# A first norm in VectorE's own chain, and half-array products of two heads in alternation

## The chip, the cores and the metric

The kernel runs on 1 core of one Trainium2 chip. The metric is the device time of one execution in microseconds (us), lower is better. The times before are the median of 3 runs.

## What is computed

One sequence of 256 tokens with 1024 features goes through two transformer blocks in float32. The parts that matter here:

```
x1 = x + 0.5 * g0 * swiglu(modulate(x, norm_w[0], shift, scale), w13, w2)   # first norm, first FFN
...
o = causal_mla_attention(...)      # first attention: 8 heads, value width 64, 256 tokens
...
y_a = mixer_a(qa, ka, va, ...)     # second attention: 8 heads of width 128
y_b = mixer_b(qb, kb, vb, bias)    # last attention: 4 heads x 3 dilations, width 64, with a bias table
x = x + (gate_a * y_a @ w_out_a + gate_b * y_b @ w_out_b) @ w_out
...                                # an MLP, a gated embedding, a last norm
```

modulate is `rmsnorm(x) * w * (1 + scale) + shift`, where scale and shift are products of silu(c) with the matrix w_ada. All weights, some 210 MB, are read once from HBM.

## The kernel before

A class `Plan` writes one list of steps by hand for the whole program; each engine then walks this list and issues those steps that are its own. An engine works its instructions strictly in that order and waits on semaphores. So the order of the plan is the order of each engine.

Weights come in units of 1 MB (128 x 2048 floats) into 4 slots `sb_raw`. A unit of kind "w" is split: ScalarE writes the rounded high part to `sb_ring` (step `hi`, two halves), VectorE the remainder (step `lo`), and a slot is loaded again as soon as its `lo` is done. TensorE multiplies each 128 x 128 tile in three passes (high x high, high x low, low x high). A unit of kind "ada" holds two blocks of columns of w_ada; VectorE multiplies it by `sb_csil` (silu of c) and sums into `sb_mod` (step `ada`, twice a unit, 128x1024 each, into `sb_junk`).

**The start** (`first_ffn`). ScalarE squares the 8 tiles of x (`square_0`), VectorE adds them (`sb_acc`), and between two of the squares, at the places in `SILU_AT`, ScalarE computes `silu_c` of each half of c. Then come unit 0 (ada), the norm of x (`x_norm`: TensorE sums over features; VectorE makes mean + eps in `sb_nst`; three Newton steps of 1/sqrt; two diagonal matrices in `sb_tq`), units 1 (w) and 2 (ada), and `norm_rows` (TensorE spreads the factors, ScalarE copies them to `sb_rbc`). With the argument `on_pool` true, the Newton steps and the diagonals are GpSimd's (POOL), else VectorE's. For each k of 8 follow `acol` (1 + scale times the norm's weight), `xr` = x times rbc (VectorE), `h_hi` (ScalarE, two instructions: scale and shift, then the rounded copy), `h_lo` (VectorE), and 16 tiles (48 matmuls 128x256) of TensorE. From k = 1 on each k also takes one w unit and one ada unit.

**The attentions** run in steps between tiles of other products: a step comes every `STEP_1` = 7 tiles (21 matmuls) in the first attention and every `STEP_B` = 12 tiles (36 matmuls) in the last. `in_steps` has 8 heads in four stages, and step n holds, in this order, the division of head n-1 (`normal`), scores of head n, the transposes of head n-2 (`turn_1`, `turn_pB`), and the product with values of head n-3 (`pv_1`, `pv_B`). Between these stages VectorE adds mask or bias (`masked_1`, `biased_B`), ScalarE takes the exponential and copies the transposes out of PSUM (`turned_1`, `turned_pB`). All transposes of one attention use one PSUM bank. These products are in full float32: one instruction in the code is two passes on the array. The values' products write 64 of 128 partitions (weights of 64 columns), the upper half for odd heads; scores of the last attention contract over 64 rows, again the upper half for odd heads. `load_bias(1)` brings the bias tables of heads 4 to 7 of the last attention (R<-scratch, two DMAs of 768 KB) into the place of the first ones and therefore waits for `biased_B` of head 3.

Of the kernel before, what the change touches and what calls it, by code (L numbers as in the profile page):

```python
# [20 lines left out]
LATE = 2  # L21
SILU_AT = (4, 7)
Z_SCALE = -8192.0
# [412 lines left out]
class Plan:  # L436
# [205 lines left out]
    def first_ffn(self):  # L642
# [22 lines left out]
        self.flush()  # L665
        norm = self.x_norm("f1", True)
        for _ in range(2):
            self.take_unit()
            self.flush()
        self.norm_rows(norm)  # L670
        bk = [b.take() for b in B]
        for k in range(8):
            if k > 1:
                self.take_unit()
                self.flush()
            if k:
# [36 lines left out]
    def mixer_1(self):  # L713
# [158 lines left out]
        def attention():  # L872
            for src in range(2):
                for hp in range(4):
# [4 lines left out]
                    done(b, ("turned", src, hp))  # L879
            p_b, pt_b, o_bank = {}, {}, [None]  # L880

# [17 lines left out]
            def pv(h):  # L899
                if h % 2 == 0:  # L900
                    o_bank[0] = B[7].take()
                pt = pt_b.pop(h)
                self.add("pv_1", h, o_bank[0], pt)
                done(pt, ("pv_1", h))
                if h % 2:
                    self.add("o_hi_1", h // 2, o_bank[0])
                    self.fill()
                    self.add("o_lo_1", h // 2, o_bank[0])
                    done(o_bank[0], ("o_1", h // 2))

# [60 lines left out]
    def mixer_2(self):  # L971
# [111 lines left out]
        def attention_b():  # L1083
            def scores(n):
                b, s, p = B[4 + n % 2].take(), tmp.take(), tmp.take()
                self.add("scores_B", n, b)
                self.add("biased_B", n, b, s)
                done(b, ("biased_B", n))
                self.add("exp_B", n, s, p)
                done(s, ("exp_B", n))  # L1090
                p_b[n] = p
                if n == 3:
                    self.add("load_bias", 1)

            o_bank = [None]

            def pv(n):
                t, s = divmod(n, 4)
                if s == 0:
                    o_bank[0] = B[7].take()  # L1100
                pt = pt_b.pop(n)
                self.add("pv_B", n, o_bank[0], pt)
                done(pt, ("pv_B", n))
# [261 lines left out]
class Tensor(Program):  # L1365
# [202 lines left out]

    def pv_1(self, h, o_bank, pt):
        m, e = self.m, self.e  # L1570
        if h % 2 == 0:
            self.turn(o_bank)
            e.wait_ge(*self.at("v_out", 1))
        e.wait_ge(*self.at("turned_1", h))
        o = o_bank.ap[64 * (h % 2):64 * (h % 2) + 64, :]
        e.matmul(o[:, 0:256], m.v1(0)[:, 64 * h:64 * h + 64], pt.ap[:, 0:256], True, False)
        e.matmul(o[:, 128:256], m.v1(1)[:, 64 * h:64 * h + 64], pt.ap[:, 256:384], False, True).then_inc(
            *self.up("pv1_ready", ("pv_1", h)))

# [72 lines left out]

    def scores_b(self, n, b):
        m, e = self.m, self.e
        t, s = divmod(n, 4)
        self.turn(b)
# [3 lines left out]
        rows = slice(64 * (s % 2), 64 * (s % 2) + 64)  # L1660
        for g in range(3):
            a = 2 * g + s // 2
            k = m.KB()[rows, a, :] if g == 0 else m.KB()[rows, a, 128 * t:128 * t + 128]
            o = b.ap[:, 0:256] if g == 0 else b.ap[:, 128 + 128 * g:256 + 128 * g]
            ins = e.matmul(o, m.QB()[rows, a, 128 * t:128 * t + 128], k, g == 0, True)
        ins.then_inc(*self.up("scoresB_ready", ("scores_B", n)))
# [8 lines left out]

    def pv_b(self, n, o_bank, pt):
        m, e = self.m, self.e
        t, s = divmod(n, 4)
        if s == 0:
# [3 lines left out]
        e.wait_ge(*self.at("turned_pB", n))  # L1683
        c = 256 * (s // 2) + 128 * t
        o = o_bank.ap[64 * (s % 2):64 * (s % 2) + 64, c:c + 128]
        vs = [m.vB(0)[:, 64 * s:64 * s + 64], m.vB(1)[:, 64 * s:64 * s + 64],
              m.vB(t)[:, 64 * (4 + s):64 * (4 + s) + 64], m.vB(t)[:, 64 * (8 + s):64 * (8 + s) + 64]]
        for i in range(4):
            ins = e.matmul(o, vs[i], pt.ap[:, 128 * i:128 * i + 128], i == 0, i == 3)
        ins.then_inc(*self.up("pvB_ready", ("pv_B", n)))  # L1690
# [76 lines left out]
class Scalar(Program):  # L1767
# [61 lines left out]
    def h_hi(self, k):  # L1829
        m, e = self.m, self.e  # L1830
        xr = m.reg(44 + k, 256)
        e.wait_ge(*self.at("xr", k))
        e.wait_ge(*self.at("acol", 0, k))
        e.wait_ge(*self.at("ada", k))
        e.activation(xr, xr, FN.Identity, scale=m.acol[:, k:k + 1], bias=m.mod[:, k:k + 1]).then_inc(
            *self.up("scalar_own"))
        e.wait_ge(*self.last())
        e.activation(m.hk(k)[0], xr).then_inc(*self.up("h_hi", ("h_hi", k)))

# [161 lines left out]
    def o_hi_1(self, hp, bank):  # L2001
        e = self.e
        e.wait_ge(*self.at("pv_1", 2 * hp + 1))
        e.activation(self.m.pair(28 + 2 * hp)[0], bank.ap[:, 0:T]).then_inc(*self.up("o_hi", ("o_hi_1", hp)))
# [103 lines left out]
    def o_hi_b(self, t, o):  # L2108
        m, e = self.m, self.e
        c = slice(128 * t, 128 * t + 128)  # L2110
        e.wait_ge(*self.at("pv_B", 4 * t + 3))
        e.activation(m.OB(0)[:, :, c], o.ap.rearrange("p (a n) -> p a n", a=2)[:, :, c]).then_inc(
# [103 lines left out]
class Vector(Elementwise):  # L2216
# [117 lines left out]

# [423 lines left out]
    def biased_b(self, n, b, s):  # L2758
# [4 lines left out]
        e.wait_ge(*self.at("bias", t, 1))  # L2763
        e.wait_ge(*self.at("scores_B", n))
        for g in range(3):
# [329 lines left out]
```

## Time and profile before

| | before |
|---|---|
| median of 3 runs | 1047.17 us (1046.88 to 1048.25) |
| the profiled execution | 1046.66 us, of which 1044.5 us are its span |
| PE (TensorE) busy | 1004.4 us, 96% |
| DVE (VectorE) busy | 758.7 us, 73% |
| ACT (ScalarE) busy | 533.8 us, 51% |
| POOL (GpSimd) busy | 17.5 us |
| DMA | 215.09 MB |

The span runs from the first to the last instruction of the profiled execution. Times in the rows below are us from the span's start; PEld is TensorE's loading of weights.

### The profile page before, as it was taken

How to read it: one execution, taken by the hardware profiler on the slowest of the kernel's cores; microseconds unless marked ns; L12 is line 12 of the kernel's file. 1: busy time of each engine (PE TensorE's matmuls, PEld its weight loads, DVE VectorE, ACT ScalarE, POOL GpSimd, SP SyncE). 2: the span in 40 equal slices, each digit the busy share in tenths (PEclk: the TensorE clock that was granted, in tenths of full speed). 3: DMA queues.
4: the chain of work that ended last, by engine and by line, in shares of the span. 5: the costliest groups of instructions: out<-in, count | busy, mean ns of one | idle time of the engine just before them, and what ended most of it. 6: DMA issues, size and time to landing. Idle time of an engine off the chain costs nothing.

```text
span 1044.5 us, 18951 instructions
## 1 busy us (share of the span) xinstructions
PE 1004.4 (96%) x7848; PEld 969.2 (93%) x7848; DVE 758.7 (73%) x1387; ACT 533.8 (51%) x920; POOL 17.5 (2%) x47
## 2 busy tenths in 40 slices
PE   2999999998889999999999999999999999999996
PEld 1999999997887999999999988799899999999996
DVE  4978998878976787685775598547568855565675
ACT  4544654436376555354564445655345654355443
POOL 2000000003000000000000000000000000000000
PEclk9999999999999999999999999999999999999998
DMA  8878899764573554678765436356554554556411
GB/s 332 321 288 304 310 353 353 291 200 163 177 267 121 201 200 165 240 230 214 249 225 193 163 121 220 140 156 172 140 181 161 178 196 166 198 181 208 152 68 41
DMA packets 34532, 215.09 MB, mean 206 GB/s; under 512 B 3725, under 2 KB 7693, under 8 KB 9614
## 3 DMA queue, kind: packets, MB, share of 16 engines
q1 hardware_dynamic: 34446, 213.88, 59.3%
q8 instruction: 62, 1.02, 0.4%
q14 instruction: 24, 0.20, 0.1%
HBM read 211.25 MB, written 2.62 MB: 205 GB/s over the span
## 4 chain that ended last, share of the span: by engine, by line
PE 85%; DVE 6%; ACT 4%; DMA 2%; issue 2%; POOL 2%; SPq 0%; DVEq 0%; ACTq 0%; POOLq 0%
PE bank L210 83%; PE bank L213 1%; DVE sb_ring L189 1%; ACT sb_ring L186 1%; ACT sb_tmp L186 1%; DMA R<-scratch 1%; ACT R L186 1%; DVE sb_tq L189 1%; DVE sb_tmp L189 1%; DVE sb_junk L198 1%; DVE sb_tmp L195 0%; POOL sb_nst L189 0%; DMA sb_x<-xt 0%; DMA sb_raw<-wts 0%; DVE sb_tmp L198 0%
## 5 line engine op out<-in xcount | busy, mean ns | idle before, releaser
L210 PE MATMUL bank<-sb_h,sb_ring 128*128 128x256 f32 (+2 forms) x4224 | 521.4, 284 | 8.1 <-DVE sb_ring L189 4.1
L210 PEld LDWEIGHTS bank<-sb_h,sb_ring 128*128 128x128 f32 (+1 forms) x4224 | 511.2, 189 | 12.1 <-issue 5.3
L189 DVE TENSOR_TENSOR sb_ring<-sb_raw,sb_ring 128x1024 fp32r<-128x1024 f32 x322 | 385.0, 1211 | 3.9 <-ACT sb_ring L186 3.8
L186 ACT ACTIVATE sb_ring<-sb_raw 128x1024 fp32r<-128x1024 f32 x322 | 319.8, 1042 | 108.6 <-PE bank L210 60.5
L210 PE MATMUL bank<-R_512r,sb_ring 128*128 128x256 f32 x1920 | 234.6, 283 | 0.0
L210 PEld LDWEIGHTS bank<-R_512r,sb_ring 128*128 128x128 f32 x1920 | 231.0, 189 | 0.8 <-issue 0.7
L189 DVE TENSOR_TENSOR sb_tq<-bank,sb_rbc 128x256 f32<-128x256 f32 x107 | 43.0, 421 | 95.0 <-PE bank L210 52.3
L198 DVE CUSTOM_DVE_ANT_0 sb_junk<-sb_raw,sb_csil,sb_cols 128x1024 bf16<-128x1024 f32 x72 | 92.3, 1281 | 1.8
L210 PE MATMUL bank<-R_1024r,sb_ring 128*128 128x256 f32 x768 | 91.5, 281 | 0.0
L210 PEld LDWEIGHTS bank<-R_1024r,sb_ring 128*128 128x128 f32 x768 | 91.3, 188 | 0.0
L210 PE MATMUL bank<-sb_ring,sb_h 128*128 128x512 f32 (+1 forms) x384 | 89.8, 387 | 0.0
L210 PEld LDWEIGHTS bank<-sb_ring,sb_h 128*128 128x128 f32 x384 | 68.1, 188 | 13.5
L186 ACT ACTIVATE R_512r<-sb_tq 128x256 fp32r<-128x256 f32 x60 | 25.1, 418 | 77.4 <-DVE sb_tq L189 50.3
L186 ACT ACTIVATE sb_tmp<-bank 128x512 f32<-128x512 f32 (+2 forms) x46 | 25.6, 561 | 41.2 <-PE bank L210 38.1
L186 ACT ACTIVATE sb_tmp<-sb_tmp,sb_smx 128x256 f32<-128x256 f32 (+2 forms) x40 | 20.9, 524 | 44.3 <-DVE sb_smx L198 33.9
L189 DVE TENSOR_TENSOR sb_tmp<-sb_tmp 128x512 f32<-128x512 f32 (+2 forms) x24 | 15.3, 638 | 31.4 <-ACT sb_tmp L186 31.2
L186 ACT ACTIVATE sb_h<-sb_x,sb_cols 128x256 fp32r<-128x256 f32 x24 | 14.2, 592 | 43.6 <-DVE sb_x L195 21.9
L195 DVE SCALAR_TENSOR_TENSOR sb_x<-bank,sb_gcol,sb_x 128x256 f32<-128x256 f32 x24 | 11.6, 482 | 34.2 <-PE bank L210 34.1
L186 ACT ACTIVATE sb_tq<-sb_tq,sb_zb 128x256 f32<-128x256 f32 x26 | 13.3, 510 | 32.3 <-DVE sb_tq L189 32.3
L189 DVE TENSOR_TENSOR R_512r<-sb_tq,R_512r 128x256 fp32r<-128x256 f32 x60 | 25.2, 420 | 3.9 <-ACT R_512r L186 3.9
L213 PE MATMUL bank<-sb_con,sb_tmp 128*128 128x128 f32 (+1 forms) x134 | 21.3, 277 | 5.2 <-ACT sb_tmp L186 3.0
L210 PE MATMUL bank<-R,R 128*128 128x256 f32 (+5 forms) x114 | 24.9, 344 | 0.0
(152 smaller groups left out, 546.8 us busy)
## 6 DMA issues: line engine op xcount, KB each, us to landing
sb_raw<-wts SPq DMA_DIRECT2D x194, 1024.0 KB, 5.1
R<-scratch SPq DMA_DIRECT2D x4, 768.0 KB, 7.8
scratch<-R SPq DMA_DIRECT2D x1, 1536.0 KB
sb_x<-xt SPq DMA_DIRECT2D x2, 512.0 KB, 5.3
out<-R SPq DMA_DIRECT2D x2, 512.0 KB, 2.9
sb_raw<-wts SPq DMA_DIRECT2D x1, 768.0 KB, 4.3
sb_raw<-wts SPq DMA_DIRECT2D x1, 640.0 KB, 4.2
sb_raw<-wts SPq DMA_DIRECT2D x1, 512.0 KB, 3.6
```

Source lines behind the costliest of these rows:

```text
L186: return Issued(self.e and self.e.activation(o, i, func, **kw))
L189: return Issued(self.e and self.e.tensor_tensor(*a))
L195: return Issued(self.e and self.e.scalar_tensor_tensor(*a))
L198: return Issued(self.e and self.e.tensor_tensor_reduce(*a))
L210: return Issued(self.e and self.e.matmul(o, w, m, start=start, stop=stop, skip_group_check=True))
L213: return Issued(self.e and self.e.transpose(o, i, ident))
```

## The change

Three things change, and the program computes the same.

First, the start. `x_norm("f1")` is called without `on_pool`, so the Newton steps and diagonals of the first norm are VectorE's; unit 2 (ada) is taken after k = 0 and no longer before `norm_rows`; `silu_c` comes ahead of square 0 and square 3; `xr` multiplies by `acol` too, `h_hi` is one instruction that only adds the shift, and `h_lo` adds the shift again before it subtracts.

```diff
-SILU_AT = (4, 7)
+SILU_AT = (0, 3)
...
-        norm = self.x_norm("f1", True)
-        for _ in range(2):
-            self.take_unit()
-            self.flush()
+        norm = self.x_norm("f1")
+        self.take_unit()
+        self.flush()
         self.norm_rows(norm)
...
-            if k > 1:
+            if k:
                 self.take_unit()
                 self.flush()
-            if k:
                 self.take_unit()
...
     def h_hi(self, k):
-        e.activation(xr, xr, FN.Identity, scale=m.acol[:, k:k + 1], bias=m.mod[:, k:k + 1]).then_inc(
-            *self.up("scalar_own"))
-        e.wait_ge(*self.last())
-        e.activation(m.hk(k)[0], xr).then_inc(*self.up("h_hi", ("h_hi", k)))
+        e.activation(m.hk(k)[0], m.reg(44 + k, 256), FN.Identity, bias=m.mod[:, k:k + 1]).then_inc(
+            *self.up("h_hi", ("h_hi", k)))
...
     def xr(self, k):
-        e.tensor_tensor(m.reg(44 + k, 256), m.x[:, k, :], m.rbc, ALU.mult).then_inc(*self.up("xr", ("xr", k)))
+        e.scalar_tensor_tensor(m.reg(44 + k, 256), m.x[:, k, :], m.acol[:, k:k + 1], m.rbc, ALU.mult,
+                               ALU.mult).then_inc(*self.up("xr", ("xr", k)))
...
     def h_lo(self, k):
-        e.tensor_tensor(lo, m.reg(44 + k, 256), hi.bitcast(F32), ALU.subtract).then_inc(
-            *self.up("h_lo", ("h", "f1", k)))
+        e.scalar_tensor_tensor(lo, m.reg(44 + k, 256), m.mod[:, k:k + 1], hi.bitcast(F32), ALU.add,
+                               ALU.subtract).then_inc(*self.up("h_lo", ("h", "f1", k)))
```

Second, `pv_1` and `pv_B` are issued for two heads at once, in the odd head's place (steps 4, 6, 8 and 10), and alternate between the two halves of columns.

```diff
             def pv(h):
-                if h % 2 == 0:
-                    o_bank[0] = B[7].take()
-                pt = pt_b.pop(h)
-                self.add("pv_1", h, o_bank[0], pt)
-                done(pt, ("pv_1", h))
                 if h % 2:
+                    o = B[7].take()
+                    pts = [pt_b.pop(h - 1), pt_b.pop(h)]
+                    self.add("pv_1", h // 2, o, pts)
...
-        for i in range(4):
-            ins = e.matmul(o, vs[i], pt.ap[:, 128 * i:128 * i + 128], i == 0, i == 3)
+        for i in range(4):
+            v = m.vB(i if i < 2 else t)
+            for side, pt in enumerate(pts):
+                s = 2 * a + side + (0 if i < 2 else 4 * (i - 1))
+                ins = e.matmul(o_bank.ap[64 * side:64 * side + 64, c:c + 128], v[:, 64 * s:64 * s + 64],
+                               pt.ap[:, 128 * i:128 * i + 128], i == 0, i == 3)
```

Third, `scores_B` is issued for two heads at once, in the even head's place (steps 0, 2, 4 and 6), into two banks, and alternates between the halves of rows.

```diff
             def scores(n):
-                b, s, p = B[4 + n % 2].take(), tmp.take(), tmp.take()
-                self.add("scores_B", n, b)
+                if n % 2 == 0:
+                    s_b.update({n: B[4].take(), n + 1: B[5].take()})
+                    self.add("scores_B", n // 2, s_b[n], s_b[n + 1])
+                b, s, p = s_b.pop(n), tmp.take(), tmp.take()
...
         for g in range(3):
+            i = 2 * g + a
+            for side, b in enumerate(banks):
+                rows = slice(64 * side, 64 * side + 64)
...
+                ins = e.matmul(o, m.QB()[rows, i, 128 * t:128 * t + 128], k, g == 0, True)
```

VectorE's instructions at the start, before, from the last row of unit 0's `ada` (`ISA sb_mod`) to the low part of h for k = 0:

```order
L198 ISA sb_mod 128x1
L192 TENSOR_SCALAR sb_nst<-bank 128x2
L189 TENSOR_TENSOR sb_ring<-sb_raw,sb_ring 128x1024 x2
L198 ISA sb_junk,sb_mod<-sb_raw,sb_csil,sb_cols 128x1024
L198 ISA sb_mod 128x1
L198 ISA sb_junk,sb_mod<-sb_raw,sb_csil,sb_cols 128x1024
L198 ISA sb_mod 128x1
L195 SCALAR_TENSOR_TENSOR sb_acol<-sb_mod,sb_cols 128x1
L189 TENSOR_TENSOR R_256_53<-sb_x,sb_rbc 128x256
L189 TENSOR_TENSOR sb_h<-R_256_53,sb_h 128x256
```

And VectorE in the same place with the change (R_256_53 is the product of `xr` for k = 0):

```order
L192 TENSOR_SCALAR sb_nst<-bank 128x2
L192 TENSOR_SCALAR sb_nst<-sb_nst 128x2
L189 TENSOR_TENSOR sb_nst<-sb_nst 128x2 x2
L195 SCALAR_TENSOR_TENSOR sb_nst<-sb_nst 128x2
L189 TENSOR_TENSOR sb_nst<-sb_nst 128x2 x2
L195 SCALAR_TENSOR_TENSOR sb_nst<-sb_nst 128x2
L189 TENSOR_TENSOR sb_nst<-sb_nst 128x2 x2
L195 SCALAR_TENSOR_TENSOR sb_nst<-sb_nst 128x2
L192 TENSOR_SCALAR sb_tq<-sb_con,sb_nst 128x128 x2
L189 TENSOR_TENSOR sb_ring<-sb_raw,sb_ring 128x1024 x2
L195 SCALAR_TENSOR_TENSOR sb_acol<-sb_mod,sb_cols 128x1
L195 SCALAR_TENSOR_TENSOR R_256_53<-sb_x,sb_acol,sb_rbc 128x256
```

The ten small instructions of 1/sqrt and the two diagonals came in ahead of unit 1's `lo`, and the two `ada` of unit 2 went out of this place (to behind k = 0).

TensorE's instructions in steps 3 and 4 of the last attention, before (R_1536_101 and R_1536_102 are the keys and queries of `scores_B`, `L213` the transposes of `turn_pB`, R_768_103 and R_768_104 the values of `pv_B`, the others the tiles between the steps):

```order
L210 MATMUL bank<-R_1536_101,R_1536_102 128x256
L210 MATMUL bank<-R_1536_101,R_1536_102 128x128 x2
L213 MATMUL bank<-sb_con,sb_tmp 128x128 x4
L210 MATMUL bank<-sb_tmp,R_768_103 64x128
L210 MATMUL bank<-sb_tmp,R_768_104 64x128
L210 MATMUL bank<-sb_tmp,R_768_103 64x128 x2
L210 MATMUL bank<-R_512r,sb_ring 128x256 x12
L210 MATMUL bank<-sb_h,sb_ring 128x256 x24
L210 MATMUL bank<-R_1536_101,R_1536_102 128x256
L210 MATMUL bank<-R_1536_101,R_1536_102 128x128 x2
L213 MATMUL bank<-sb_con,sb_tmp 128x128 x4
```

TensorE in steps 3 and 4 with the change:

```order
L213 MATMUL bank<-sb_con,sb_tmp 128x128 x4
L210 MATMUL bank<-R_512r,sb_ring 128x256 x12
L210 MATMUL bank<-sb_h,sb_ring 128x256 x24
L210 MATMUL bank<-R_1536_101,R_1536_102 128x256 x2
L210 MATMUL bank<-R_1536_101,R_1536_102 128x128 x4
L213 MATMUL bank<-sb_con,sb_tmp 128x128 x4
L210 MATMUL bank<-sb_tmp,R_768_103 64x128 x2
L210 MATMUL bank<-sb_tmp,R_768_104 64x128 x2
L210 MATMUL bank<-sb_tmp,R_768_103 64x128 x4
```

Step 3 keeps its transposes alone; step 4 has the scores of heads 4 and 5 and the values' products of heads 0 and 1. Head 3's scores moved from step 3 to step 2.

## Rows read from the trace of the kernel before

**Rows 1.** Page, part 1: busy time, share and instructions of each engine.

```profile
PE 1004.4 (96%) x7848; PEld 969.2 (93%) x7848; DVE 758.7 (73%) x1387; ACT 533.8 (51%) x920; POOL 17.5 (2%) x47
```

**Rows 2.** Timeline of the start, all engines: start, duration, engine, what.

```profile
11.00 1.28 DVE L198 CUSTOM_DVE_ANT_0 sb_junk<-sb_raw,sb_csil,sb_cols 128x1024 bf16<-128x1024 f32 x1
...
13.39 2.00 ACT L186 ACTIVATE sb_ring<-sb_raw 128x1024 fp32r<-128x1024 f32 x2 [2.43 <-DMA sb_raw<-wts]
...
13.53 0.15 DVE L192 TENSOR_SCALAR sb_nst<-bank 128x2 f32<-128x2 f32 x1
...
14.48 2.36 DVE L189 TENSOR_TENSOR sb_ring<-sb_raw,sb_ring 128x1024 fp32r<-128x1024 f32 x2 [0.80 <-ACT sb_ring L186]
...
21.26 0.73 POOL L192 TENSOR_SCALAR sb_tq<-sb_con,sb_nst 128x128 f32<-128x128 f32 x2 [0.18 <-POOL sb_nst L189]
...
21.68 1.22 PE L210 MATMUL bank<-sb_tq,sb_con 128*128 128x128 f32 x4 [8.68 <-POOL sb_tq L192]
22.94 0.38 ACT L186 ACTIVATE sb_rbc<-bank 128x256 f32<-128x256 f32 x1 [7.55 <-PE bank L210]
...
24.52 0.42 ACT L186 ACTIVATE sb_h<-R 128x256 fp32r<-128x256 f32 x1
...
24.97 0.43 DVE L189 TENSOR_TENSOR sb_h<-R,sb_h 128x256 fp32r<-128x256 f32 x1 [1.11 <-ACT sb_h L186]
...
25.50 36.67 PE L210 MATMUL bank<-sb_h,sb_ring 128*128 128x256 f32 x289 [2.59 <-issue]
```

**Rows 3.** Windows: busy us (instructions) of PE, PEld, DVE, ACT, POOL; PEclk; DMA; GB/s.

```profile
25.50:29.86 4.36, 4.36 (x20) 4.36 (x21) 4.21 (x7) 4.14 (x6) 0.00 (x0) 1.00 0.11 26
...
33.50:45.00 11.50, 11.50 (x98) 11.50 (x98) 11.36 (x19) 5.92 (x9) 0.00 (x0) 1.00 0.99 371
```

**Rows 4.** Timeline of VectorE in the next norm: first and last of its chain.

```profile
402.70 0.16 DVE L192 TENSOR_SCALAR sb_nst<-bank 128x2 f32<-128x2 f32 x1 [0.55 <-PE bank L210]
...
404.86 0.48 DVE L192 TENSOR_SCALAR sb_tq<-sb_con,sb_nst 128x128 f32<-128x128 f32 x2
```

**Rows 5.** Groups by shape, VectorE: count, busy us, mean ns.

```profile
L195 DVE SCALAR_TENSOR_TENSOR sb_h<-sb_x,sb_acol,sb_h 128x256 fp32r<-128x256 f32 x16 | 7.7, 483 | 7.4 <-ACT sb_h L186 7.3
```

**Rows 6.** Timeline of TensorE, last attention: scores, step 5's transposes, last product.

```profile
707.16 1.14 PE L210 MATMUL bank<-R,R 64*128 64x256 f32 x6
...
712.69 1.14 PE L210 MATMUL bank<-R,R 64*128 64x256 f32 x6
...
718.24 1.14 PE L210 MATMUL bank<-R,R 64*128 64x256 f32 x6
...
724.15 1.14 PE L210 MATMUL bank<-R,R 64*128 64x256 f32 x6
...
731.30 1.14 PE L210 MATMUL bank<-R,R 64*128 64x256 f32 x6
...
740.30 0.66 PE L213 MATMUL bank<-sb_con,sb_tmp 128*128 128x128 f32 x4 [0.72 <-ACT sb_tmp L186]
...
766.85 1.09 PE L210 MATMUL bank<-sb_tmp,R 128*64 128x128 f32 x8 [0.16 <-ACT sb_tmp L186]
```

**Rows 7.** Timeline of TensorE in the first attention, steps 4 and 6.

```profile
321.20 0.55 PE L213 MATMUL bank<-sb_con,sb_tmp 128*128 128x128 f32 x3 [0.80 <-ACT sb_tmp L186]
321.68 0.86 PE L210 MATMUL bank<-sb_tmp,R 128*64 128x256 f32 x4
322.47 2.78 PE L210 MATMUL bank<-sb_h,sb_ring 128*128 128x258 f32 x21
...
330.68 0.55 PE L213 MATMUL bank<-sb_con,sb_tmp 128*128 128x128 f32 x3 [0.28 <-ACT sb_tmp L186]
```

**Rows 8.** Timeline of ScalarE ahead of step 5 of the first attention.

```profile
324.99 0.17 ACT L186 ACTIVATE sb_zb<-bank 128x1 f32<-128x1 f32 x1 [1.15 <-PE bank L210]
```

**Rows 9.** Timeline of the DMA queue (SPq): the second load of bias.

```profile
727.07 1.28 SPq L216 DMA_DIRECT2D R<-scratch  x2
```

**Rows 10.** Timeline of VectorE: the first use of that bias.

```profile
737.28 0.61 DVE L198 CUSTOM_DVE_ANT_1 sb_tmp<-bank,R 128x256 f32<-128x256 f32 x1 [5.04 <-DMA R<-scratch]
```

More of the change, by code:

```diff
@@ L879, in attention @@
                     done(b, ("turned", src, hp))
-            p_b, pt_b, o_bank = {}, {}, [None]
+            p_b, pt_b = {}, {}
             def scores(h):
@@ L899, in pv @@
             def pv(h):
-                if h % 2 == 0:
-                    o_bank[0] = B[7].take()
-                pt = pt_b.pop(h)
-                self.add("pv_1", h, o_bank[0], pt)
-                done(pt, ("pv_1", h))
-                if h % 2:
-                    self.add("o_hi_1", h // 2, o_bank[0])
+                if h % 2:
+                    o = B[7].take()
+                    pts = [pt_b.pop(h - 1), pt_b.pop(h)]
+                    self.add("pv_1", h // 2, o, pts)
+                    for pt in pts:
+                        done(pt, ("pv_1", h // 2))
+                    self.add("o_hi_1", h // 2, o)
                     self.fill()
-                    self.add("o_lo_1", h // 2, o_bank[0])
-                    done(o_bank[0], ("o_1", h // 2))
+                    self.add("o_lo_1", h // 2, o)
+                    done(o, ("o_1", h // 2))
             yield from in_steps(scores, lambda h: self.add("normal_1", h, p_b[h]), turn, pv)
@@ L1093, in scores @@
                     self.add("load_bias", 1)
-            o_bank = [None]
+            o_bank, s_b = [None], {}
             def pv(n):
@@ L1100, in pv @@
                     o_bank[0] = B[7].take()
-                pt = pt_b.pop(n)
-                self.add("pv_B", n, o_bank[0], pt)
-                done(pt, ("pv_B", n))
+                if s % 2:
+                    pts = [pt_b.pop(n - 1), pt_b.pop(n)]
+                    self.add("pv_B", n // 2, o_bank[0], pts)
+                    for pt in pts:
+                        done(pt, ("pv_B", n // 2))
                 if s == 3:
@@ L1567, in turn_1, with pv_1 @@
         e.transpose(b.ap[:, 256:384], p.ap[:, 128:256], m.ident).then_inc(*self.up("p1_turned", ("turn_1", h)))
-    def pv_1(self, h, o_bank, pt):
+    def pv_1(self, hp, o, pts):
         m, e = self.m, self.e
[L1571 to L1578, printed above, removed]
+        self.turn(o)
+        e.wait_ge(*self.at("v_out", 1))
+        e.wait_ge(*self.at("turned_1", 2 * hp + 1))
+        for part in range(2):
+            for i, pt in enumerate(pts):
+                h, a = 2 * hp + i, o.ap[64 * i:64 * i + 64, :]
+                if part == 0:
+                    e.matmul(a[:, 0:256], m.v1(0)[:, 64 * h:64 * h + 64], pt.ap[:, 0:256], True, False)
+                else:
+                    ins = e.matmul(a[:, 128:256], m.v1(1)[:, 64 * h:64 * h + 64], pt.ap[:, 256:384], False, True)
+        ins.then_inc(*self.up("pv1_ready", ("pv_1", hp)))
     def branch(self, f, k, bank):
@@ L1651, in pv_a, with scores_b @@
             *self.up("pvA_ready", ("pv_A", h)))
-    def scores_b(self, n, b):
+    def scores_b(self, n, *banks):
         m, e = self.m, self.e
-        t, s = divmod(n, 4)
-        self.turn(b)
+        t, a = divmod(n, 2)
+        self.turn(*banks)
         for what in ("kB0", "kqB", "qB0"):
@@ L1659, in scores_b @@
             e.wait_ge(*self.at("turned_2", (what, 1)))
-        rows = slice(64 * (s % 2), 64 * (s % 2) + 64)
         for g in range(3):
[L1662 to L1665, printed above, removed]
+            i = 2 * g + a
+            for side, b in enumerate(banks):
+                rows = slice(64 * side, 64 * side + 64)
+                k = m.KB()[rows, i, :] if g == 0 else m.KB()[rows, i, 128 * t:128 * t + 128]
+                o = b.ap[:, 0:256] if g == 0 else b.ap[:, 128 + 128 * g:256 + 128 * g]
+                ins = e.matmul(o, m.QB()[rows, i, 128 * t:128 * t + 128], k, g == 0, True)
         ins.then_inc(*self.up("scoresB_ready", ("scores_B", n)))
@@ L1674, in turn_pb, with pv_b @@
         ins.then_inc(*self.up("pB_turned", ("turn_pB", n)))
-    def pv_b(self, n, o_bank, pt):
+    def pv_b(self, n, o_bank, pts):
         m, e = self.m, self.e
-        t, s = divmod(n, 4)
-        if s == 0:
+        t, a = divmod(n, 2)
+        if a == 0:
             self.turn(o_bank)
@@ L1682, in pv_b @@
             e.wait_ge(*self.at("vB_out", "v1", 1))
[L1683 to L1687, printed above, removed]
-        for i in range(4):
-            ins = e.matmul(o, vs[i], pt.ap[:, 128 * i:128 * i + 128], i == 0, i == 3)
+        e.wait_ge(*self.at("turned_pB", 2 * n + 1))
+        c = 256 * a + 128 * t
+        for i in range(4):
+            v = m.vB(i if i < 2 else t)
[3 more added lines that the diff above has]
+                               pt.ap[:, 128 * i:128 * i + 128], i == 0, i == 3)
         ins.then_inc(*self.up("pvB_ready", ("pv_B", n)))
@@ L2002, in o_hi_1 @@
         e = self.e
-        e.wait_ge(*self.at("pv_1", 2 * hp + 1))
+        e.wait_ge(*self.at("pv_1", hp))
         e.activation(self.m.pair(28 + 2 * hp)[0], bank.ap[:, 0:T]).then_inc(*self.up("o_hi", ("o_hi_1", hp)))
@@ L2110, in o_hi_b @@
         c = slice(128 * t, 128 * t + 128)
-        e.wait_ge(*self.at("pv_B", 4 * t + 3))
+        e.wait_ge(*self.at("pv_B", 2 * t + 1))
         e.activation(m.OB(0)[:, :, c], o.ap.rearrange("p (a n) -> p a n", a=2)[:, :, c]).then_inc(
@@ L2325, in xr @@
         e.wait_ge(*self.at("rbc", "f1"))
-        e.tensor_tensor(m.reg(44 + k, 256), m.x[:, k, :], m.rbc, ALU.mult).then_inc(*self.up("xr", ("xr", k)))
+        e.wait_ge(*self.at("acol", 0, k))
+        e.scalar_tensor_tensor(m.reg(44 + k, 256), m.x[:, k, :], m.acol[:, k:k + 1], m.rbc, ALU.mult,
+                               ALU.mult).then_inc(*self.up("xr", ("xr", k)))
     def h_lo(self, k):
@@ L2763, in biased_b @@
         e.wait_ge(*self.at("bias", t, 1))
-        e.wait_ge(*self.at("scores_B", n))
+        e.wait_ge(*self.at("scores_B", n // 2))
         for g in range(3):
```

2 lines of the change are left out of this document (removed).

## The prediction

> **What bounds the kernel now.** I read the page first, then a table of windows, then the timeline at the three changed places. TensorE is busy for 1004.4 of 1044.5 us [rows 1], so the end moves by what TensorE's stream gains or loses, and by nothing else. Some 40 us are idle for TensorE, and the largest single stretch is the start: its main products begin at 25.50 [rows 2] and from then on run without a gap through the first FFN. That start is the one place where another engine's chain counts in full. In the attentions the question is of two sorts: how long TensorE's own half-array blocks take, and whether it then stands before a result that is not there yet.
>
> **The start, before.** The chain is to be seen in [rows 2]. VectorE is through with unit 0's two ada and makes the variance at 13.53. GpSimd then takes until 21.26 to come to the diagonals. TensorE's spread at 21.68 had waited for them, ScalarE copies rbc at 22.94, and xr, two instructions of h_hi (the last at 24.52) and h_lo (24.97 to 25.40) follow. Meanwhile unit 1's lo (14.48) was long done.
>
> **The start, after.** What comes first stays where it is. Putting silu ahead lets the squares end earlier, but unit 1 lands only at 13.39 (ScalarE had waited 2.43 for it), units land one behind another, and at 371 GB/s [rows 3] a unit of 1.05 MB takes 2.8 us; so unit 0 lands at 10.6 or a little later, and its first ada can't start much ahead of the 11.00 of before. The variance stays at 13.5. I give silu's move 0, with at most 0.4 to gain.
> - VectorE's chain: in the next norm it is 2.16 us from the variance to the first diagonal (402.70 to 404.86), and 0.48 for both [rows 4]. So the first diagonal is at 15.7 and VectorE is free at 16.2.
> - Unit 1's lo: ScalarE has finished hi at 15.4, so lo runs from 16.1 for 2.36, to 18.5. The spread and rbc take from 21.68 to 23.32 before [rows 2], 1.64 us; after, they end at 17.4, beside lo. So lo is the longer of the two branches.
> - acol 0.1, xr as a three-operand instruction 0.48 [rows 5], h_hi 0.42 to 0.6, h_lo 0.48, and some 0.15 us of handing over: 1.65 us. TensorE begins at 20.15, against 25.50. This term is -5.35 us.
> - Does TensorE then keep going? Its first 20 matmuls took 4.36 us, 0.218 each, and later ones 98 in 11.50, 0.117 [rows 3], or, over the whole row of 289 in 36.67 us [rows 2] less these, 0.120; I take 0.119 for each. The granted clock reads 1.00 in both rows, so the row doesn't name the cause; the first pitch fits the lower of the two levels, 1.2 GHz, since TensorE had done nothing for 2.59 us before it. I expect this slow beginning again, unchanged, since it stands idle for some 3 us again. The 48 matmuls of k = 0 then end at 20.15 + 4.4 + 28 x 0.119 = 27.9. VectorE until then: ada twice 2.65, acol 0.1, xr 0.45, lo 2.3, h_lo 0.45, about 5.85 with what overlaps taken off, from 20.05 to 25.9. There are 2 us of slack at k = 1, where before unit 2 had been taken in advance. VectorE runs gapless there already (11.36 of 11.50 us) at TensorE's pace. Two three-operand instructions cost 0.06 us each more for every k, 0.12 x 7 = 0.8 us, less than the 2 us. DMA has its units issued in the same relation to their use as in the later k. So nothing is given back; if the slack failed, up to 2 us would be.
>
> **The half-array blocks.** In the last attention the distances in [rows 6] give each block's net cost. Scores and 36 matmuls: 712.69 - 707.16 = 5.53; 36 x 0.119 is 4.28, so scores of one head cost 1.25. With transposes 724.15 - 718.24 = 5.91, so these cost 0.38 to 0.44. With the values' product 731.30 - 724.15 = 7.15, so it costs 1.24. The product is 8 passes in 1.09 us, the last one's latency of some 0.3 included, so a pass of 128 columns takes 0.11 and one of 256 some 0.215. Pure passes are thus 0.88 of 1.24 and 0.87 of 1.25: about 0.37 us of each visit is spent on going from the whole array to half of it and back. In the first attention a product takes 0.79 from start to start (321.68 to 322.47 in [rows 7]), and 0.95 with what it costs on both sides.
>
> Two heads in one visit save 0.37 each time, a sure thing: 12 visits fewer, 4.4 us of TensorE time. The unknown is whether passes of different halves run at the same time. No row shows two halves back to back. Bounds: none, then a pair's passes take 1.74 (scores), 1.76 (values, last) or 1.30 (values, first); or full, with each head's second pass beside the other's first: 9 slots of 0.11 = 1.0 for 16 passes, 0.75 for the first attention; for scores I take 1.2, since a matrix of 128 columns must be loaded for each pass at the pitch of 0.117 that PEld shows [rows 3]. I take full, since the two heads' passes share no operand and write other partitions or another bank.
>
> The Trainium skill ("TensorEngine Tiling (Array Packing)", Key Properties) says that changing the tiling mode drains the engine and changing the tile alone doesn't, and that tiles can load and multiply in parallel; this agrees with the 0.37 us of a visit. But "TensorE: Matmul & The Clock Gate" (Part 3, The mechanism) says that a weight load overlaps with matmuls in flight only when the row group differs. Column halves share their rows, so by this rule alone only the scores would gain, and the sum would be 1041.0 instead of 1036.9.
>
> **What of this reaches the end.** First attention. Step 3 loses its product (-0.95), but at step 4 the transposes already wait 0.80 for ScalarE [rows 7], whose work up to there was released before step 3's product; so this goes into a wait of 1.75. Step 5 loses one, and step 6 waits already (0.28), behind ScalarE work that begins at 324.99, before step 5 [rows 8]; lost too. Steps 7 and 9 show no such wait, and their 1.9 us are gained, but for some 0.3 at step 9's transposes. The four pairs cost 0.37 + 0.75 = 1.1 against 0.95, +0.1 each. Sum: -1.2 us (+0.6 without overlap, when each pair costs 0.65 more than one product).
>
> Last attention. A pair of scores costs 0.4 + 1.2 = 1.6, a pair of products 0.35 + 1.0 = 1.35. From 707.16: step 1 at 713.05, step 2 at 717.35, step 3 at 723.7, step 4 at 728.45, step 5 at 736.1. But the second bias load stands there: issued at 727.07 [rows 9], used at 737.28, VectorE having waited 5.04 for it [rows 10], and ScalarE frees the transposes' bank only behind exp of that head, so TensorE's transposes of step 5 already wait 0.72, until 740.30. That load goes out after head 3's bias, which VectorE can add 0.9 us earlier (its scores are there), and takes its 10.2 us in any case. So the transposes come at 739.35: TensorE now waits 3.2 us, and of all that was won up to there only 0.95 reaches the end. From there: step 6 at 744.2, step 7 at 751.9, step 8 at 756.6, step 9 at 761.3. The last product needs ScalarE's copy of step 9's transposes, and waits for it before too (0.16 at 766.85 [rows 6]); transposes, copy and handing over come to some 1.8 us, so it starts at 763.1 and ends at 764.1, against 766.85 + 1.02 = 767.9. Sum: -3.75 us. Without overlap the same steps give 767.9, that is 0.
>
> **Sum.** -5.35 - 1.2 - 3.75 = -10.3 us against the profiled 1046.66, or 1036.4. The median of the runs is 0.5 above the profiled time: 1036.9.
>
> **The rivals.**
> - No overlap of halves at all: -5.35 + 0.6 + 0 = -4.75, 1042.4. For it: every pass in the rows keeps to 0.11, however small its half. Against it: nothing in the rows forces two halves into one queue. 0.18.
> - Row halves overlap and column halves don't, because the load of one head's 64 columns waits until the other head's pass is through: -5.35 + 0.6 - 1.4 (the bias load is met at the same 739.35, three pairs of products cost 0.8 more each) = -6.1, 1041.0. For it: products go through all 128 rows for both heads. Against it: 64-column loads are as hidden in the rows as others. 0.12. It is what the Trainium skill's rule in "TensorE: Matmul & The Clock Gate" (Part 3, The mechanism) would give.
> - The start gives most back: TensorE reaches k = 1 before VectorE does, or its slow beginning lasts longer because it has less work ahead. It costs 2 to 5 of the 5.35 us; with overlap 1040. For it: VectorE is busy 11.36 of 11.50 us. Against: the 2 us of slack. 0.08.
> - TensorE is slow again after the 3.2 us wait at step 5, as it is after its wait at 25.50: another 20 matmuls at 0.218, +2.0, 1038.9; inside the likeliest case's range.
> - Slower than before: going from half to half costs as much as going from whole to half, some 0.1 to 0.2 us. The pairs have 4 x (3 + 7 + 5) = 60 such changes. The -4.75 us of the case without overlap are used up at 0.08 us for each change; at 0.2 it is +7.3, 1054.4. Against it stands that a load of 64 columns for the next pass is already hidden within a visit. 0.04.
>
> **How the numbers follow.** The likeliest case, full overlap, has a chance of 0.58 and a range of its own of 1034.5 to 1039.5 (start 1.5 either way, the waits 1 either way, the slow stretch +2). The range reaches on to the cases without overlap, to 1042.7; above lie the slower case and a part of the third. Faster by over 0.2% (2.1 us, about what a measurement here can tell from nothing): 0.94. Within 0.2%: 0.02. Slower: 0.04.
>
> **What would show it.** In the profile of the changed kernel: no GpSimd row before 25 us; the variance at 13.5 and the first diagonal 2.2 us later; the first 128x256 matmul at 20 to 20.5, and none waiting for sb_ring or sb_h up to 60. A pair of values' products (16 passes) that starts and ends within 1.3 us, not 2.0; a pair of scores (12 passes) within 1.5, not 1.95. Steps 4 and 6 of the first attention with waits of 1.7 and 1.2 us for ScalarE, and step 5 of the last with 3 us behind R<-scratch. It is wrong if the pairs take the sum of their passes, if the first matmul comes after 21, or if TensorE starves at k = 1.

## The result, and the profile after

Before: 1047.03 us (median of 4 runs, 1046.35 to 1048.25). After: 1037.66 us (median of 4 runs, 1036.80 to 1038.82). The ratio is 0.9913, with a 95% interval of 0.9901 to 0.9924: 9.4 us faster. The profiled execution took 1037.56 us, with a span of 1035.8. The forecast was 1036.9. The single steps are off by more than the sum, as the rows show.

The page's line of busy times, which answers to [rows 1]:

```profile
span 1035.8 us, 18934 instructions
PE 993.6 (96%) x7848; PEld 962.9 (93%) x7848; DVE 761.8 (74%) x1399; ACT 528.8 (51%) x911; POOL 10.5 (1%) x32
```

TensorE issues as many matmuls as before and is busy 10.8 us less. The start, on the timeline of all engines, which answers to [rows 2] (start, duration, engine, line, operation; in brackets the idle time before it and what ended it):

```profile
10.69 1.28 DVE L198 CUSTOM_DVE_ANT_0 sb_junk<-sb_raw,sb_csil,sb_cols 128x1024 bf16<-128x1024 f32 x1 [0.36 <-DMA sb_raw<-wts]
...
13.23 0.15 DVE L192 TENSOR_SCALAR sb_nst<-bank 128x2 f32<-128x2 f32 x1
...
15.46 0.48 DVE L192 TENSOR_SCALAR sb_tq<-sb_con,sb_nst 128x128 f32<-128x128 f32 x2
...
15.86 2.35 DVE L189 TENSOR_TENSOR sb_ring<-sb_raw,sb_ring 128x1024 fp32r<-128x1024 f32 x2
17.06 0.38 ACT L186 ACTIVATE sb_rbc<-bank 128x256 f32<-128x256 f32 x1 [1.93 <-PE bank L210]
...
18.95 0.51 ACT L186 ACTIVATE sb_h<-R,sb_mod 128x256 fp32r<-128x256 f32 x1 [1.51 <-DVE R L195]
...
19.49 0.49 DVE L195 SCALAR_TENSOR_TENSOR sb_h<-R,sb_mod,sb_h 128x256 fp32r<-128x256 f32 x1 [0.58 <-ACT sb_h L186]
...
20.08 1.19 PE L210 MATMUL bank<-sb_h,sb_ring 128*128 128x256 f32 x4 [3.06 <-DVE sb_h L195]
```

GpSimd is gone from the stretch, 2.23 us lie between the variance and the first diagonal, unit 1's lo outlasts rbc, and the first main product is at 20.08, 5.42 us earlier. From xr to the first main product it is 1.65 us (18.43 to 20.08), and was 2.07 (23.43 to 25.50): of the 5.42 us, 0.42 come from the fewer instructions for h, and 5.00 from the chain ahead of xr. From the first main product to 233 us TensorE's record has no distance between two starts above 0.6 us: k = 1 doesn't starve it.

TensorE's timeline of the first attention (step 4 and step 6), answering to [rows 7], and of the last one, answering to [rows 6]:

```profile
315.68 0.55 PE L213 MATMUL bank<-sb_con,sb_tmp 128*128 128x128 f32 x3 [1.77 <-ACT sb_tmp L186]
316.16 0.87 PE L210 MATMUL bank<-sb_tmp,R 128*64 128x256 f32 x8
316.96 2.78 PE L210 MATMUL bank<-sb_h,sb_ring 128*128 128x258 f32 x21
...
325.16 0.55 PE L213 MATMUL bank<-sb_con,sb_tmp 128*128 128x128 f32 x3 [1.27 <-ACT sb_tmp L186]
...
700.53 1.15 PE L210 MATMUL bank<-R,R 64*128 64x256 f32 x12
...
722.65 1.09 PE L210 MATMUL bank<-sb_tmp,R 128*64 128x128 f32 x16
723.67 3.11 PE L210 MATMUL bank<-R_512r,sb_ring 128*128 128x256 f32 x24
726.62 1.58 PE L210 MATMUL bank<-sb_h,sb_ring 128*128 128x256 f32 x12
732.93 1.11 PE L213 MATMUL bank<-sb_con,sb_tmp 128*128 128x128 f32 x4 [4.73 <-ACT sb_tmp L186]
...
740.21 1.15 PE L210 MATMUL bank<-R,R 64*128 64x256 f32 x12
...
758.29 1.09 PE L210 MATMUL bank<-sb_tmp,R 128*64 128x128 f32 x16 [1.17 <-ACT sb_tmp L186]
759.31 3.11 PE L210 MATMUL bank<-sb_h,sb_ring 128*128 128x256 f32 x24
```

A pair now takes what one head took: 16 passes in 1.09 us where 8 took 1.09 [rows 6], 12 in 1.15, 8 in 0.87. But at step 5 TensorE stands idle for 4.73 us. VectorE's timeline shows the bias load behind it, and the table of windows what TensorE does ahead of it and afterwards, with the start's first matmuls in the first row (length; busy time and instructions of PE, PEld, DVE, ACT, POOL; granted clock; DMA share; GB/s):

```profile
729.84 0.60 DVE L198 CUSTOM_DVE_ANT_1 sb_tmp<-bank,R 128x256 f32<-128x256 f32 x1 [7.21 <-DMA R<-scratch]
```

```profile
20.08:24.60 4.52, 4.52 (x21) 4.52 (x22) 4.41 (x8) 1.78 (x3) 0.00 (x0) 1.00 0.80 274
...
726.00:728.10 2.10, 2.10 (x19) 2.00 (x17) 0.00 (x0) 0.00 (x0) 0.00 (x0) 1.00 1.22 230
731.54:738.37 6.83, 5.44 (x26) 5.44 (x27) 5.37 (x14) 4.89 (x9) 0.00 (x0) 0.50 0.34 114
732.90:737.50 4.60, 4.57 (x22) 4.57 (x23) 3.55 (x10) 2.77 (x4) 0.00 (x0) 0.50 0.32 91
732.93:740.21 7.28, 7.28 (x41) 7.15 (x41) 4.20 (x12) 3.53 (x6) 0.00 (x0) 0.63 0.41 146
```

Ahead of the wait at step 5 19 matmuls are under way in 2.10 us, at a granted clock of 1.00; behind it 22 take 4.57 at 0.50, which is 1.2 of 2.4 GHz. The clock fell at 731.54, while TensorE stood idle, and was back at 1.00 at 738.37. From the transposes to the next scores it takes 7.28 us. The 1.00 of the first row is no measurement: the trace's own records of the clock begin only at 24.98 us (before: 29.79), where the half pace of the start ends, and the table reads a stretch without a record as 1.00.

Where the 8.7 us of span come from, as shifts of TensorE's milestones: first main product -5.42; first attention's scores at 297.36 against 302.62; the attention itself 43.18 us against 45.01 (-1.83); 0.46 lost between the attentions; the last attention 58.78 against 60.71 (-1.93). The rest are hundredths on the way. The 0.46 come from a gap near 476 us in which TensorE starts nothing for 0.86 us; the profile names no releaser for it. The profiled executions of three kernels below have it too (0.7 to 0.9) and those of the kernel before and of six others don't, with and without the change; its cause stays open.

### The profile page after: what moved, and what is told of

It is laid out like the page before. It is cut to its first block, busy times and chain, and to the rows that moved or that the text cites. A ratio compares the mean times of both kernels' runs of the same rounds, so it can differ in the third digit from the quotient of the medians.

```text
span 1035.8 us, 18934 instructions
## 1 busy us (share of the span) xinstructions
PE 993.6 (96%) x7848; PEld 962.9 (93%) x7848; DVE 761.8 (74%) x1399; ACT 528.8 (51%) x911; POOL 10.5 (1%) x32
## 4 chain that ended last, share of the span: by engine, by line
PE 82%; DVE 8%; ACT 4%; DMA 3%; issue 2%; POOL 1%; SPq 0%; DVEq 0%; ACTq 0%; POOLq 0%
PE bank L210 81%; DVE sb_ring L189 2%; DMA R<-scratch 2%; PE bank L213 1%; ACT sb_ring L186 1%; DMA sb_raw<-wts 1%; ACT sb_tmp L186 1%; DVE sb_tmp L198 1%; DVE sb_tq L189 1%; ACT R L186 1%; DVE sb_tmp L189 1%; DVE sb_junk L198 1%; DVE sb_tmp L192 0%; DVE sb_tmp L195 0%; POOL sb_st_a L189 0%
## 5 line engine op out<-in xcount | busy, mean ns | idle before, releaser
L210 PEld LDWEIGHTS bank<-sb_ring,sb_h 128*128 128x128 f32 x384 | 68.1, 188 | 13.5
L213 PE MATMUL bank<-sb_con,sb_tmp 128*128 128x128 f32 (+1 forms) x134 | 21.7, 281 | 11.1 <-ACT sb_tmp L186 8.9
L213 PEld LDWEIGHTS bank<-sb_con,sb_tmp 128*128 128x128 f32 (+1 forms) x134 | 15.9, 143 | 15.9 <-ACT sb_tmp L186 9.6
```

The costliest lines, as they stand in the source:

```text
L210: return Issued(self.e and self.e.matmul(o, w, m, start=start, stop=stop, skip_group_check=True))
L213: return Issued(self.e and self.e.transpose(o, i, ident))
```

## Experiments

All are compared with the kernel before on the same chip.

**The start alone.** The kernel before with the whole first change: the norm in VectorE's chain, unit 2's ada later, silu ahead, fewer instructions for h. A cut of it:

```diff
-        norm = self.x_norm("f1", True)
-        for _ in range(2):
-            self.take_unit()
-            self.flush()
+        norm = self.x_norm("f1")
+        self.take_unit()
+        self.flush()
...
```

> The kernel before with the change at the start alone. Theory: the gain at the start is worth its full 5.4 us at the end, since TensorE has no gap behind it through the first FFN: first 128x256 matmul at 20.1 and 1041.6 us (ratio 0.9948). Rival: a part is given back later, where TensorE meets the same waits earlier (transfers keep their time): 1042.5 to 1044, with the loss seen at the start of the first or the last attention.

1040.86 us, ratio 0.9942 (0.9927 to 0.9957): 5.7 us faster, and 5.2 in span. First main product at 20.48, last attention 5.28 us earlier than before. Little is given back: the last attention takes 61.00 us instead of 60.71, with a wait of 1.00 instead of 0.72 at step 5.

**The pairs alone.** The changed kernel with the start's edits undone (the whole first change the other way round).

> The changed kernel with the start as it was before. Theory: the parts add, so this one has 1.8 us from the first attention and 1.9 from the last, and 0.4 to 1.3 that the 1.2 us of shift between them showed: 1043.3 to 1043.7 us (ratio 0.9967). First matmul back at 25.5, the wait for the second bias load at step 5 of the last attention still 4.5 to 5 us, and a slow stretch of TensorE behind it. Rival: part of what looked like the pairs' gain is the earlier start's, because transfers and other engines are then ahead: 1045 or more.

1043.56 us, ratio 0.9968 (0.9955 to 0.9981): 3.0 us faster. The first attention takes 43.47 us, the last 57.55; the wait at step 5 is 4.47, and from the transposes behind it to the next scores it takes 6.31. The first matmul, expected back at 25.5, comes at 26.41: in this execution VectorE's first ada already starts at 11.82 instead of 11.00, so the shift is there ahead of everything that the edit reaches, and no run names its cause. The two gains, 5.7 and 3.0, add to 8.7 of the 9.4, within what the intervals leave open.

**Two ada ahead of the norm's rows.**

```diff
         norm = self.x_norm("f1")
-        self.take_unit()
-        self.flush()
+        for _ in range(2):
+            self.take_unit()
+            self.flush()
         self.norm_rows(norm)
...
```

> The changed kernel, but with unit 2's ada taken on VectorE ahead of the first norm's rows, as before the change. Theory (with the norm in VectorE's own queue, whatever stands ahead of it there counts in full): two ada of 1.3 us each push the first 128x256 matmul from 20.08 to 22.7, and the time to 1040.3 us. Rival (unit 1's lo by VectorE, 15.86 to 18.2, is the longer branch anyway, and TensorE meets VectorE again at k = 1, where the ada taken early are missing): first matmul later, but less than 1 us lost at the end, 1038.5.

VectorE's and TensorE's rows on the timeline:

```profile
18.22 1.28 DVE L198 CUSTOM_DVE_ANT_0 sb_junk<-sb_raw,sb_csil,sb_cols 128x1024 bf16<-128x1024 f32 x1
...
22.71 2.69 PE L210 MATMUL bank<-sb_h,sb_ring 128*128 128x256 f32 x11 [5.59 <-DVE sb_h L195]
```

The first product comes 2.63 us later, as the theory said, and at 233 to 236 us and at the first attention's scores (299.65 against 297.36) TensorE is still 2.3 us behind the changed kernel. The time is 1039.22 (ratio 0.9923, 0.9906 to 0.9939), between the two forecasts and, beside 0.9913, not clearly apart from the changed kernel; this execution lacks the gap near 476 us that the changed kernel's has, and that hides 0.8 of the 2.3. The trace decides for the theory, the time of the runs alone would not.

**Silu at its old place.** One line, `SILU_AT = (4, 7)`.

> The changed kernel with silu at its old place behind the squares. Theory: the first ada starts at 11.0 instead of 10.7, and the first matmul at 20.4 instead of 20.08; +0.3 us. Rival (unit 0's landing sets the first ada, silu is early enough in both): the first matmul at 20.1.

The first ada starts at 10.87, the first product at 20.25, in one execution that took 1036.11. Kernels with silu ahead and the same start have it at 19.86 to 20.48. The 0.17 us to the changed kernel are within that scatter, so no effect can be told: 0 in the forecast fits.

**The pairs not alternated.** Same visits, the second head's matmuls behind all of the first's (shown for the last attention's products; scores and the first attention's products alike):

```diff
         for i in range(4):
-            v = m.vB(i if i < 2 else t)
-            for side, pt in enumerate(pts):
+        for side, pt in enumerate(pts):
+            for i in range(4):
+                v = m.vB(i if i < 2 else t)
...
```

> The changed kernel with the two heads' passes issued one head after the other within the same visit: same matmuls, same visits, only the order differs. Theory (the halves run side by side only because neighbouring passes lie in different halves): 16 passes take 1.76 us instead of 1.09, 12 passes of scores 1.7 instead of 1.15, 8 passes 1.3 instead of 0.87. In the first attention some 1.3 us come back, in the last 2.5 behind the wait for the bias load, which itself shrinks from 4.73 to some 3: 1041 to 1042 us. Rival (the order doesn't matter, the second head's passes slide beside the first's anyway, or only the fewer visits bring the gain): blocks as short as in the changed kernel and 1037.7 us.

TensorE's timeline, and the table of windows: three moments of 10 ns in a pair of products, for TensorE's matmuls of line 210 alone, and for all engines the stretch behind the wait:

```profile
315.55 0.88 PE L210 MATMUL bank<-sb_tmp,R 128*64 128x256 f32 x8
...
720.73 1.68 PE L210 MATMUL bank<-R,R 64*128 64x256 f32 x12
722.34 0.66 PE L213 MATMUL bank<-sb_con,sb_tmp 128*128 128x128 f32 x4
722.93 1.58 PE L210 MATMUL bank<-sb_tmp,R 128*64 128x128 f32 x16
...
732.29 0.66 PE L213 MATMUL bank<-sb_con,sb_tmp 128*128 128x128 f32 x4 [3.32 <-ACT sb_tmp L186]
```

```profile
723.30:723.31 0.01, 0.01 (x3) 1.00 1.02 205
723.75:723.76 0.01, 0.01 (x5) 1.00 1.85 308
724.20:724.21 0.01, 0.01 (x2) 1.00 0.53 102
...
732.29:738.67 6.38, 6.38 (x40) 6.24 (x40) 4.18 (x12) 3.54 (x6) 0.00 (x0) 0.73 0.49 167
```

Products of the last attention take 1.58 instead of 1.09 us and scores 1.68 instead of 1.15, while the first attention's products keep 0.88. The order matters, then, but not fully. A pass is under way for about 0.27 us, and one starts every 0.11 where a head runs alone; so 2 or 3 are under way at the first and third moment, as with one head, and 5 at the second, as with two. The single records say where the second head comes in: five passes start 0.11 us apart, then one at 723.42, 5 ns behind the fifth, with the longer duration (0.32 us) that the first pass of a row of such products has, and from there two rows of starts run side by side until 723.80. So the second head's first pass starts beside the first head's fifth, four places behind it in program order and ahead of its sixth to eighth. With scores (six passes a head) the same happens beside the third pass, at 721.27, which is four places too; and in the first attention (four passes a head) the second head starts 13 ns behind the first. A block of four passes per head thus loses nothing, one of eight loses 0.49 us. The records don't name the head of a pass: this is the reading that fits all three blocks.

The time, 1039.01 us (ratio 0.9929, 0.9912 to 0.9945), is lower than forecast and not clearly apart from the changed kernel; the trace shows the loss, 60.59 us for the last attention instead of 58.78. The first attention lost 0.03 us, not 1.3 (43.21 against 43.18), and behind the wait of 3.32 the stretch is shorter, 6.38 us instead of 7.28, since the clock is at 0.50 for 3.41 us and not for 6.83. The shorter wait isn't shown to be the reason: the kernel with the pairs alone waited 4.47 and has 3.41, too:

```profile
738.59:742.00 3.41, 3.23 (x15) 3.23 (x16) 2.90 (x8) 2.41 (x4) 0.00 (x0) 0.50 0.19 31
```

**Two matmuls of each head in turn**, in the last attention's products:

```diff
-        for i in range(4):
-            v = m.vB(i if i < 2 else t)
-            for side, pt in enumerate(pts):
+        for j in range(8):
+            i, side = 2 * (j // 4) + j % 2, j // 2 % 2
+            pt, v = pts[side], m.vB(i if i < 2 else t)
...
```

> The changed kernel with the values' products of the last attention in another order: two matmuls (four passes) of the one head, then two of the other, and so on, where the changed kernel alternates after each matmul. Not alternated at all, 16 passes took 1.58 us, and the other head's first pass began beside the first head's fifth, four places ahead of its own turn; the first attention's blocks of four passes lost nothing (0.88 against 0.87). Theory (a pass can start beside one that stands up to four places ahead of it, if it has the other half): 16 passes take 1.09 us again. Rival (column halves need strict alternation): 1.2 to 1.4 us.

```profile
721.62 1.15 PE L210 MATMUL bank<-sb_tmp,R 128*64 128x128 f32 x16
```

16 passes take 1.15 us (1036.88 in one execution), 0.06 above strict alternation and under the rival's range of 1.2 to 1.4. Runs of four passes are nearly free.

**The second bias load cut by head.** Each head's part of it goes out once that head's first bias has been added, instead of all of it behind head 3:

```diff
-                if n == 3:
-                    self.add("load_bias", 1)
+                if n < 4:
+                    self.add("load_bias", 1, n)
...
-            e.wait_ge(*self.at("biased_B", 3))
+            e.wait_ge(*self.at("biased_B", head))
...
+                hs = slice(head, head + 9, 4)
+                e.dma_start(m.bias()[64 * i:64 * i + 64, hs, :], rows[:, hs, s:s + 256]).then_inc(
+                    *self.up(f"bias{i}_h{head}_in", ("bias", t, i, head), by=16))
```

> The changed kernel with the second bias load cut into one load for each head of the first half, issued as soon as that head's bias has been added, instead of one for all behind head 3. Theory (the 4.73 us wait at step 5 is this load's, and TensorE's slow stretch behind it, 2.4 us, is the wait's consequence): both go, the last attention takes some 53 us instead of 58.8, and the time is 1031 to 1033 us. Rival A: another engine's chain (ScalarE's exponentials) is right behind the load, so only 1 to 2 us are gained: 1036. Rival B: the slow stretch does not hang on the wait and stays: 1035.

TensorE's timeline around step 5, and that stretch in the table of windows:

```profile
726.29 1.59 PE L210 MATMUL bank<-sb_h,sb_ring 128*128 128x256 f32 x12
727.71 0.60 PE L213 MATMUL bank<-sb_con,sb_tmp 128*128 128x128 f32 x4
...
732.52 1.15 PE L210 MATMUL bank<-R,R 64*128 64x256 f32 x12
...
751.62 3.11 PE L210 MATMUL bank<-sb_h,sb_ring 128*128 128x256 f32 x24
```

```profile
727.71:732.52 4.81, 4.81 (x43) 4.67 (x41) 3.87 (x11) 2.52 (x5) 0.00 (x0) 1.00 0.41 118
```

No wait and no slow stretch: the last attention takes 51.42 us instead of 58.78, and the time is 1029.84 (ratio 0.9838, 0.9823 to 0.9853), another 7.8 us below the changed kernel. 4.73 of them are the wait and 2.47 (7.28 - 4.81) the slow stretch; both rivals fall. This kernel beats the one before and the changed one.

**The same cut in the kernel before.**

> The kernel before with the second bias load cut by head. Theory (that load cost TensorE only 0.72 us there): 0.7 to 1 us less than before, 1045.7 (ratio 0.9992), so within what can be told from no change; the load became expensive only once the pairs made the attention shorter. Rival (the load's contention with the weights costs something everywhere): 3 us or more less than before.

1046.14 us, ratio 0.9986 (0.9976 to 0.9995): 1.5 us less, of which the last attention shows 0.78 (59.93 against 60.71), which is about the wait of 0.72 [rows 6]. Once the pairs are in, the same edit takes 7.36 us off the last attention.

**The wait filled.** In place of standing idle, TensorE multiplies the identity by itself (36 passes, added work) ahead of step 5's transposes:

```diff
+    def idle_b(self, o):
+        for _ in range(18):
+            self.e.matmul(o.ap[:, 128:256], self.m.ident, self.m.ident, True, True)
...
```

> The changed kernel with 18 more matmuls of the identity by itself (36 passes, some 4 us) on TensorE where it otherwise stands idle before step 5 of the last attention; they write columns of the output bank that the first half doesn't use and the second half overwrites. The wait for the transposed tile's bank stays as long as it is, only TensorE is busy in it. Theory (TensorE is slow behind that wait because it stood idle): from the transposes to the next scores it takes some 4.9 us instead of 7.28, at a granted clock of 1.00, and the time is 1035.3 us (ratio 0.989), 2.4 us less than the changed kernel although it does more. Rival (the slow stretch comes from what runs there, or from the bias load's traffic): the stretch stays at 7.3 us and the time at 1037.7 or above.

TensorE's timeline and the table of windows:

```profile
726.94 4.18 PE L210 MATMUL bank<-sb_con 128*128 128x128 f32 x36
731.53 0.66 PE L213 MATMUL bank<-sb_con,sb_tmp 128*128 128x128 f32 x4 [0.41 <-ACT sb_tmp L186]
```

```profile
731.53:736.40 4.87, 4.87 (x41) 4.74 (x41) 3.53 (x10) 3.06 (x6) 0.00 (x0) 1.00 0.39 113
```

The transposes come hardly sooner (32.11 us behind the first scores, against 32.40), but behind them the clock is 1.00 and the stretch takes 4.87 us. 1034.74 us, ratio 0.988 (0.9864 to 0.9897): 2.9 us less than the changed kernel with more work, of which the trace shows 2.41 in this stretch and 0.29 ahead of it. TensorE's idleness made it slow; the rivals (what runs there, the load's traffic) fall, for both are still there and the stretch is short.

## Why the prediction was nearly right

The median is 0.8 us above the forecast. That it is so near is partly luck: errors of both signs cancelled, +2.4 for the slow stretch against -0.6 and -0.8 for cheaper pairs.

- **The start: right, -5.42 for -5.35.** The variance at 13.23 instead of 13.5 (the first ada starts as soon as unit 0 has landed), lo to 18.2 for 18.5, and the slow first 20 matmuls came again. The clock column's 1.00 in the first of [rows 3], which the prediction took for a reading, means only that the trace holds no record there.
- **Pairs overlap: right, and the term was mis-sized.** I put a pair of scores at 1.6 us net, of products at 1.35 and 1.1. A pair of scores costs what one head's cost: from 700.53 to 710.34 is 9.81, less 72 x 0.119 is 1.24. Weight loads of either shape didn't hold the passes up. By this the first attention gained 1.83 and not 1.2 (four pairs, some 0.15 less each), and the last 0.80 more behind step 6 (19.10 us from its scores to the end for 19.9).
- **Column halves like row halves.** The Trainium skill says in "TensorE: Matmul & The Clock Gate" (Part 3, The mechanism) that a weight load overlaps matmuls in flight only when the row group differs. The rows disagree: products go through all 128 rows for both heads, and 16 passes took the 1.09 us of 8. The rival at 1041.0 that followed from it is refuted. [rows 1] spoke against it already: matmuls are busy 96% and weight loads 93% of the span, nearly all of both through the same 128 rows. The same section says that matmuls start strictly in program order; the unalternated pair, where a pass of the second head seems to start ahead of three of the first, speaks against it.
- **The waits of the first attention: right,** 1.77 and 1.27 for 1.75 and 1.2.
- **The wait at step 5: right place, too small.** 4.73 for 3.2. The transposes came 0.74 earlier for 0.95: the load went out 1.8 us earlier behind the first scores, not 0.9, but took 11.2 us from issue (718.67) to use (729.84) for 10.2; and TensorE, with cheaper pairs, was there 27.67 us behind its first scores (728.20), not the 28.94 of my steps.
- **The slow stretch: the step that failed.** "TensorE is slow again after the 3.2 us wait", +2.0, stood among the rivals and belonged in the sum: it cost 2.4 us. The rows of the start had shown the same pattern, an idle 2.59 us and then half pace, and I took it as certain there and as a rival here. The kernel before had a nearer case, which the prediction doesn't use: a wait of 4.09 us in the middle of the kernel, and the clock at 0.50 around its end (TensorE's timeline, and the table of windows):

```profile
262.21 4.89 PE L210 MATMUL bank<-sb_h,sb_ring 128*128 128x258 f32 x27 [4.09 <-DVE sb_ring L189]
```

```profile
261.90:265.31 3.41, 3.10 (x14) 3.11 (x15) 3.38 (x6) 0.00 (x1) 0.00 (x0) 0.50 0.57 187
```

The last attention's -1.93 for -3.75 is thus +0.21 (the load), +2.43 (the slow stretch) and -0.80 (cheaper pairs).

- **Two sums that changed nothing.** The spread and rbc end 2.06 us behind the first diagonal before (21.26 to 23.32), not 1.64; lo was the longer branch in any case. The first attention without overlap comes to +0.7 to +1.0 by the prediction's own terms (-1.9, at most 0.3 lost, 4 x 0.65), not +0.6.

What stays open is the slow stretch's size: behind 4.4 to 4.8 us of idling it took 6.31 to 7.53 us to the next scores in five kernels, for 4.8 to 4.9 undisturbed. The clock stood at 0.50 for 3.41 us in one of them and for 6.83 in the four others; two of them idled the same 4.47 us and had one each. So the length of the wait alone doesn't set it.

## What to carry to other kernels

When a change shortens TensorE's work between a buffer's release and its next load's use, the load becomes the bound: follow it first, and cut it so that each part goes out as its part of the buffer comes free. Here that was worth nearly as much as the whole change. A wait of some microseconds on TensorE can be paid for again behind it, so price both: in this kernel waits of 3.3 to 4.8 us were followed by the lower clock, the waits of 1.0 to 1.8 us in the attentions were not. Look for such a wait in the trace at hand before forecasting. Blocks that use half of the array should be put next to blocks of the other half, in turns of at most four float32 passes.

## What the runs showed of the hardware

- Two half-array streams cost as much as one, for row and for column halves: 1.15 for 1.14 us and 1.09 for 1.09.
- Passes of the other half seem to start out of turn, beside one that stands up to four places ahead: four passes in a row of one half cost nothing or 0.06 us, eight cost 0.49.
- Behind the idle 4.73 us the granted clock was 0.50 for 6.83 us from 731.54 on, and behind a wait of 4.09 in the kernel before for 3.41 us; with the 4.73 us filled by 36 passes of no use it stayed at 1.00.
- At the start 21 matmuls took 4.52 us, the same half pace, under a clock column of 1.00 (the first row of that table of windows). The clock's own records begin at 24.98 us, where that pace ends: there the pace shows what the column can't.
